# Transposes of attention weights placed directly ahead of the next scores, in two small transformer networks on one core

## The reference

```python
def _chunk_attention(q, k, v, rel_bias):            # 8 heads of 64, biased, chunk-causal
    s = jnp.einsum('bqhd,bkhd->bhqk', q_i, k_i).astype(jnp.float32) + bias[None]
    s = jnp.where(valid[None, None, None, :], s, NEG_INF)
    p = jax.nn.softmax(s, axis=-1).astype(v.dtype)
    return jnp.einsum('bhqk,bkhd->bqhd', p, v_i)
...
    # nsa_attention: 8 query heads in 2 groups, 256 keys; o_cmp over 15 compressed keys
    ps = masked_softmax(...)                          # selected blocks (here all of them)
    o_s = jnp.einsum("bgrqnk,bgqnkd->bqgrd", ps, vg)
    sw = jnp.einsum("bqgrd,bkgd->bgrqk", qb, kw) * scale
    pw = masked_softmax(sw, mw).astype(vw.dtype)      # window
    o_w = jnp.einsum("bgrqk,bkgd->bqgrd", pw, vw)
    o = g[..., 0, None] * o_cmp + g[..., 1, None] * o_s + g[..., 2, None] * o_w
```

## Time and profile before

| | us |
|---|---|
| median of 3 runs | 1976.82 (1976.53 to 1977.29) |
| the profiled execution, its own time | 1976.44 |
| its span, from the first to the last instruction | 1974.6 |
| PE busy | 1962.4 |
| DVE busy | 1249.1 |
| ACT busy | 911.7 |

### The profile page before, as it was taken

One profiled execution on the slowest core, in us unless ns is written; L12 is line 12 of the kernel. 1 busy time (PEld: TensorE's weight loads), 2 busy tenths in 40 slices (PEclk: granted clock), 3 DMA queues, 4 the chain that ended last, 5 costly groups with the idle time before them and its releaser, 6 DMA issues.

```text
span 1974.6 us, 32204 instructions
## 1 busy us (share of the span) xinstructions
PE 1962.4 (99%) x14032; PEld 1792.9 (91%) x14032; DVE 1249.1 (63%) x1760; ACT 911.7 (46%) x1215; POOL 98.6 (5%) x84
## 2 busy tenths in 40 slices
PE   8999999999999999999999999999999999999998
PEld 7888999999888899999999989899999998989997
DVE  6566656665756666655565568665556556776555
ACT  4445444444444555444444435544444444555442
POOL 0000001000100000100010020010010002001000
PEclk9999999999999999999999999999999999999999
DMA  7544566675454455686666656369666664746663
GB/s 284 185 143 143 176 209 193 198 213 192 171 171 145 133 187 198 194 253 184 192 196 189 192 172 172 107 197 264 178 180 202 188 191 152 193 119 193 188 186 105
DMA packets 421446, 361.87 MB, mean 183 GB/s; under 512 B 29424, under 2 KB 361528, under 8 KB 421304
## 3 DMA queue, kind: packets, MB, share of 16 engines
q1 hardware_dynamic: 421160, 359.74, 59.6%
q10 hardware_dynamic: 144, 0.07, 0.0%
HBM read 358.72 MB, written 1.05 MB: 182 GB/s over the span
## 4 chain that ended last, share of the span: by engine, by line
PE 99%; DVE 0%; DMA 0%; ACT 0%; issue 0%; DVEq 0%
PE ps L218 23%; PE ps L220 23%; PE ps L219 23%; PE ps L225 8%; PE ps L227 8%; PE ps L226 8%; PE ps L1546 2%; PE ps L1722 1%; PE ps L1657 1%; PE ps L1698 1%; PE ps L1674 1%; PE ps L1711 0%; DMA cst<-in_const 0%; PE ps L1845 0%; PE ps L1762 0%; PE ps L1818 0%
## 5 line engine op out<-in xcount | busy, mean ns | idle before, releaser
L2119 DVE TENSOR_TENSOR hl<-raw,hl 128x1024 fp32r<-128x1024 f32 (+2 forms) x535 | 722.5, 1384 | 377.4 <-ACT hl L1873 377.0
L218 PE MATMUL ps<-xt,hl 128*128 128x256 f32 (+1 forms) x2672 | 754.8, 282 | 0.0
L219 PE MATMUL ps<-xt,hl 128*128 128x256 f32 (+1 forms) x2672 | 746.2, 279 | 0.0
L220 PE MATMUL ps<-xt,hl 128*128 128x256 f32 (+1 forms) x2672 | 745.7, 279 | 0.0
L1873 ACT ACTIVATE hl<-raw 128x2048 fp32r<-128x2048 f32 (+1 forms) x338 | 613.8, 1824 | 217.1 <-PE ps L227 158.1
L218 PEld LDWEIGHTS ps<-xt,hl 128*128 128x128 f32 (+1 forms) x2672 | 500.9, 187 | 7.0 <-issue 3.0
L219 PEld LDWEIGHTS ps<-xt,hl 128*128 128x128 f32 (+1 forms) x2672 | 501.0, 188 | 3.1
L220 PEld LDWEIGHTS ps<-xt,hl 128*128 128x128 f32 (+1 forms) x2672 | 500.8, 187 | 0.2
L225 PE MATMUL ps<-hl,o 128*128 128x512 f32 x656 | 261.5, 399 | 0.3
L227 PE MATMUL ps<-hl,o 128*128 128x512 f32 x656 | 259.0, 395 | 0.0
L226 PE MATMUL ps<-hl,o 128*128 128x512 f32 x656 | 258.8, 394 | 0.0
(11 more groups left out here) (211 smaller groups left out, 1555.4 us busy)
## 6 DMA issues: line engine op xcount, KB each, us to landing
raw<-in_w_in SPq DMA_DIRECT2D x83, 1024.0 KB, 5.0
raw<-in_w_ffn_in SPq DMA_DIRECT2D x88, 512.0 KB, 5.1
raw<-in_ffn_gate SPq DMA_DIRECT2D x88, 512.0 KB, 3.9
raw<-in_ffn_up SPq DMA_DIRECT2D x88, 512.0 KB, 5.2
raw<-in_ffn_down SPq DMA_DIRECT2D x44, 1024.0 KB, 5.1
raw<-in_w_ffn_out SPq DMA_DIRECT2D x22, 1024.0 KB, 5.2
raw<-in_w_out SPq DMA_DIRECT2D x24, 512.0 KB, 4.6
raw<-in_w_branch_a SPq DMA_DIRECT2D x8, 1024.0 KB, 5.3
```

The costliest lines, as they stand in the source:

```text
L218: e.matmul(out, l[0], r[0], start=start, stop=False)
L219: e.matmul(out, l[0], r[1], start=False, stop=False)
L220: return e.matmul(out, l[1], r[0], start=False, stop=stop)
L2119: e.tensor_tensor(lo[:, c], m["raw"][:, k % NRAW, 0:n][:, c], hi[:, c].bitcast(F), ALU.subtract).then_inc(s.low.up(("low", k), *([("low", ...
```

## The change

The step T no longer costs anything, and its cost (0.88 in the second network, 0.44 or 0.88 in the first) is put on the S step. By the order of `slots`, T of task n-1 is then followed at once by scale of task n and S of task n+1. In the second network T of task 1 also waits until the second part of `lin_conv` has been passed, side work gets two steps behind a costly step (over 2), a step of cost 0 stands ahead of the compressed branch's first X, and the score banks are taken without a preference.

```diff
     def score_parts(qs, ks, i, rs, q_events, read):
 
+        spare, PB.spare = PB.spare, None
         bs, ers = dense([PB.take() for _ in range(2)]), [ER.take() for _ in range(2)]
+        PB.spare = spare
         n = len(rs[0])
@@ ca_attention
-                yield 1.45 + 0.95 * i
+                yield 1.45 + 0.95 * i + 0.44 * T
                 add("scale", ers, rs, rc, None, 128 * T)
                 yield 0
                 ets = turned(ers, i)
                 full()
-                yield 0.44 * T
+                yield 0
@@ lin_conv
-            for cost in t_parts(*t_proj(w_in, 0)):
+            for n, cost in enumerate(t_parts(*t_proj(w_in, 0))):
                 yield cost
-                at.mark("q")
+                at.mark(("q", "q next")[min(n, 1)])
@@ nsa, compressed
                 yield PART if i else 0.9
+                if i == 0:
+                    yield 0
                 tb, et = PB.take(), ET.take()
                 add("cmp_turn", l, i, er, tb, et)
@@ nsa, task
-                yield SCORES
+                yield SCORES + 0.88
...
                 add("scale", ers, rs, rc, (("gates", l), gate[:, :, :, 1:3] if i == 0 else gate[:, :, :, bs[0]]), 512 // n)
                 yield 0
+                if (jp, bs) == (0, (1,)):
+                    yield from at.until("q next")
                 ets = turned(ers, 1)
-                yield 0.88
+                yield 0
                 yield from at.until("v")
@@ nsa
                 yield cost
-                x = next(side, IDLE)
-                if x is not IDLE:
-                    yield x
+                for _ in range(2 if cost > 2 else 1):
+                    x = next(side, IDLE)
+                    if x is not IDLE:
+                        yield x
                 full()
```

## The result

| | before | after |
|---|---|---|
| median, us | 1976.80 (14 runs) | 1982.33 (1979.37 to 1983.45, 14 runs) |
| ratio of the means | | 1.0024 [1.0017, 1.0031] |
| the profiled execution, us | 1976.44 | 1982.38 |
| its span | 1974.6 | 1980.6 |

The forecast was 1975.2, from 1973.0 to 1978.0. The page of after answers to the earlier trace rows: six microseconds more of span, and the same busy time of PE. The list of waits has to show idle time, and the clock whether busy time is worth the same.

The account below looks back on a forecast made before the run. PE was taken to bound the kernel, busy 1962.4 of 1974.6 us. Savings of 1.0 us in the second network and 0.6 in the first, 1.6 in sum, gave 1975.2 us against the median, range 1973.0 to 1978.0.

Parts of the forecast that it names:

- No wait is added: First network: S held two or three dense parts longer adds no wait; two layers save 0.6 us.
- The turns of the rotated queries: First network, PE: they lose S3 and V1 as neighbours and gain T2 and T3, effect 0 (0.1 either way).
- forecast 0.3: First network: T1 moves from an island of its own to S3, 0.29 us saved.
- The slower rival: ACT gates T4, V4 and the first `lin_conv2` part in the second network: 1982.8 us, chance 0.07.
- its join saves the dense borders: Second network, V2 directly ahead of T3: V gets no shorter, only two dense borders are saved, 0.20 us.
- The first output part: Second network: its weight load stands idle for 0.32 us behind a late seed on ACT; 0.28 is taken back.
- forecast 5.3: Second network: compressed values start right after X0's copy on DVE, 5.3 us after S5's end.
- a sign of the slower rival: T2, the first `lin_conv2` part or V4 starting late while ACT is still at a copy or an exponential.
- forecast 0.49: Second network, per layer: 1.54 us saved less 1.05 of added waits; 1.0 us over two layers.
- 1.05 was forecast: Second network, waits per layer: 0.9 us at the compressed values plus 0.15 for T5 and the part behind it.
- 1.54: Second network, savings per layer: 1.16 T and S joins, 0.20 V2 with T3, -0.1 side work, 0.28 output part.
- the forecast's own wait: Second network: PE waits 0.9 us a layer (0 to 1.5) at the compressed values, as DVE is late with X0's copy.

Follow-up runs that it names:

- 1975.27: The second network's edits alone, with the first network's attention keeping its old costs: 1975.27 us against 1976.63, ratio 0.9993.
- 1974.91: The whole change, but S of the first task in the first network keeps its old cost, so S1, T0 and S2 return to their places: 1974.91 us, ratio 0.9991.
- Two experiments: The second network's edits alone, plus compressed values asked for one planner turn later: 1974.88 us; or plus the convolution's gate one dense part later: 1978.93 us.
- 1974.88: The second network's edits alone, with the compressed values asked for one planner turn later, behind V3 again: 1974.88 us, ratio 0.9991.
- all ten executions: The changed kernel with only S1 of the first network's attention put back behind the 3rd dense part: 1977.52 us, ratio 1.0003.

## Why the prediction was wrong

**The step that failed** is "No wait is added: S is held for two or three dense parts more behind its predecessor, and all ends (V3) fall on the same part", in the part on the first network. It looked at the attention's own chain and at PE. What decided was a third party: DVE's queue, which S's bias and maxima and T's copies share with the `low` halves of the weight units and with the rotation. The order came out on PE as counted, 12 islands a layer for 13, T1 with S3. The turns of the rotated queries, put at "0 (0.1 either way)", cost 2.42 + 1.51 a layer in the profiled execution. Three signs of it were in the trace of before: the rotation's end 1.77 ahead of the turn, V0 and T1 ahead of that turn (0.59 and 0.39 by their starts, and some 0.2 of borders each), and ACT's `high` that runs until 134.72, which the 7th part's `low` has to wait for. With the 0.15 of the handover and the 1.22 that the changed kernel shows, the first two leave 0.4, and the kernel with S1, T0 and S2 at their places has 0.26 (0.41 less 0.15). The range missed too, for the same reason: this wait was neither a term nor a rival, and neither was a lower clock.

**The sum as it should have stood**, per layer of the first network: 2.42 of wait, 1.51 of half clock, and 0.18 saved (half of the 0.36 between 1975.27 and 1974.91; forecast 0.3): 3.75 lost. Two layers 7.5, less the 1.36 measured for the second network, gives 6.1; the profiled executions differ by 5.94. With the pause by starts (2.59) it is 6.5. Without the half clock it is 2 x 2.24 - 1.36 = 3.1, so 1979.9, and five executions of the changed kernel ran at 1979.4 to 1980.5. The 0.18 is half of a difference of medians that is hardly clear of their spread.

**The slower rival** had another mechanism, ACT as the gate at T4 and V4 and at the first `lin_conv2` part. No wait of PE stands there in after. It is ruled out, although the time came out at 1982.33 beside its 1982.8: that is chance.

**What was right**, all in the second network. T to S takes 0.49 to 0.52 in place of the 0.55 assumed. V takes 1.01 ahead of T, as ahead of dense work, so its join saves the dense borders. (The Trainium skill, TensorEngine Tiling (Array Packing), Key Properties, has a drain at any change of the tiling mode; the trace shows no more for V2 ahead of T3, 1259.49 to 1260.50, than for V3 ahead of a dense part, 1268.25 to 1269.26, both 1.01. By their tiles both are such changes, so no row here gives the price of one.) The first output part follows T4 0.64 behind its start with the 0.32 of the earlier trace rows gone. The compressed values start 5.1 behind S5's end (1262.08 to 1267.19), forecast 5.3; the wait was 0.47 and not 0.9, as DVE was 0.2 earlier and PE came to them 4.64 behind S5 (1266.72) and not 4.4. T2's wait of 0.20 for ACT has no term in the sum; the prediction has such a wait as a sign of the slower rival only. Net 0.54 a layer in the timeline, forecast 0.49. That these two are so close is partly luck: the waits came to 0.67 where 1.05 was forecast, so the savings were, by difference, 1.21 and not 1.54.

**The price of the forecast's own wait** was right as a place and wrong as something to be won back. Two experiments removed it, and DVE's lateness came out at T5 (0.59), or at T5 and the output part (0.44 and 1.66).

**What stays open.** Nothing here separates a gain of 0.1% from none with certainty: the best kernels (1974.88 and 1974.91) have intervals that end at 1.0000. That S3 waits for the rotation's bank is read from the releaser and the code; no experiment moved it. What makes the clock fall in most executions of the changed kernel and not in all isn't known.

## What to carry to other kernels

Where a change moves steps in one program order, write down, for every engine that takes part in the step, what stands between its old and its new place, above all an instruction that itself waits for a third engine; here 3.9 us of ready DVE work went behind a `low` that wasn't ready, and S1 behind one `low` more, and the rotation ended 2.8 us later, though no step became longer. Then look at every consumer with little slack on the bottleneck engine, not only at those of the moved steps: the slack at each handover (1.62 here) is in the trace of before and costs one look. Where a queue is late as a whole, moving one of its steps moves the wait and doesn't remove it.

## What the hardware showed beyond that

A wait of PE can cost more than its length. Behind 2.42 us of idle time the granted clock went from full to half in the profiled execution, and the stretch behind it took 1.51 us longer; behind 1.29 us at the same place it stayed whole in all ten executions.

The longer wait did not bring the half clock every time. The 14 times of the changed kernel lie in two groups, and the mean granted clock, which is on record for each execution, parts them in the same way: 0.998 in the nine from 1982.26 to 1983.45, and 0.999 or 1.000, as in the kernel before, in the five from 1979.37 to 1980.45. Two stretches at half clock take 2 x 4.0 x (1 - 0.57) / 1980.6 = 0.0017 off the mean by the window above, which fits. The distance of the two main values, 1979.5 and 1982.3, is about the price of the two stretches (3.0). So the lower group is most likely the wait without the half clock; a timeline of one of its executions is not on record.
